# Eight weight chunks of the second block's modulation move from the first retrieval into the first mixer, and the retrieval's entry is reordered

## The chip, the cores and the metric

The kernel runs on one core of one Trainium2 chip, as one program. The time is device time in microseconds (us). Three timed runs of the kernel before gave 2483.28, 2483.88 and 2486.16 us; the median, 2483.88, is the number to compare. All arithmetic is float32.

## The reference, cut to what matters

Two blocks work on x, 256 tokens of width 1024, and a third part (sparse attention, gated linear attention and a mixture of experts) follows; the change does not touch that part. Each of the two blocks does:

```python
m = silu(c) @ mod_w[l] + mod_b[l]            # 6144 values: sh1, sc1, g1, sh2, sc2, g2
h = rms_norm(x, norm1_g[l]) * (1 + sc1) + sh1
y = mixer(h)                                 # l = 0: attention and gated MLP; l = 1: pooling
x = x + g1 * y
h2 = rms_norm(x, norm2_g[l]) * (1 + sc2) + sh2
x = x + g2 * peer_ffn(h2, ...)               # the retrieval
```

peer_ffn makes queries h2 @ w_q (2048 wide: 8 heads of two halves), scores them against 128 keys per half, takes the best 16 of the sums per head and token, and looks those 128 experts up in tables `down` and `up` of 16384 rows. The result of a token is the sum over its experts of gate times gelu(down_row . h2) times up_row. Each of the two blocks thus fetches 256 x 128 rows of 8 KB (a down and an up row side by side), 268 MB. The modulation weights of a block are 1024 x 6144, 25 MB, read for a single vector c.

## The kernel before, in words

Every engine has its own instruction stream, written out by hand, and they meet at semaphores. Weights come through a ring of four slots of 2 MB each; SyncE (SP) issues all weight loads in one fixed order, and before each load it waits until the last user of its slot is done (`load_weight`, L564 to L571). Which chunk goes to which slot is laid down by `stream(tag, chunks, used, places)`: `places` picks from the list `turn` of slots; without it the slot used longest ago is taken.

First comes a head (to 62 us) with four chunks of the first block's modulation. In the mixer the other eight chunks of that block are multiplied with silu(c) by `row_parts` (L2036): 16 instructions a chunk that put the chunk's result into row r of bank 7, where the rows add up in one accumulation. `cwin` is a window of zeros with c in one column; shifting it picks the row. VectorE then adds the bias rows to bank 7 (`mrows`, L1352), and eight matmuls with `rows_of(r)` (L2160) spread each row over the 128 partitions, from where ScalarE copies them to `mod`. Around it TensorE does the projections (`in_tiles`), attention in four iterations (scores1, turn1, value1) and the gated MLP; then `transposes` and `project_out1`, four products (two tiles of 128 tokens by two column halves) into banks 4 to 7.

`peer(0)` is the first retrieval. VectorE adds a tile to x (`add_tile`) and normalises it (`start`, with ScalarE's sum of squares and root, `enter`), tile 0 then tile 1. TensorE transposes a tile (`turn`), makes the query of the first two heads halved (`first_query`, `first_scores`), and then query products numbered s, each cut in four `quarter`s of 16 instructions and followed by `scores(s)`; number s stands for column chunk s // 2 and tile s % 2. Before the loop it does s = 1 and three quarters of s = 2. VectorE finds the top 16 in 15 steps (`top_k`); after head 0 the Pool engine starts fetching (L678), one indirect DMA for each expert number and tile: 128 tokens, 1 MB. There are 256 of them for each retrieval and eight buffers, four in the arena and two in each of two ring slots lent for the time (`lend`); number 6 waits for query product 1, and from number 8 on each pair waits until the matmuls of its buffer are done. For each pair VectorE makes two dot products (L1424), ScalarE applies gelu and the gate and builds two diagonal matrices (L888 to L897), and TensorE adds diagonal times up rows into the output banks (L2250), eight instructions. The quarters left over are spread over the first groups of this loop.

The second block's modulation is computed inside the retrievals: ten chunks in the first, two in the second (`HIDDEN`), one per block of eight pairs. `mod_parts` multiplies a chunk into bank 4 or 5, ScalarE copies it to `mpart`, `mod_total` sums over partitions and adds the bias, ScalarE copies it to `mod`. SyncE loads these chunks in between, waiting for the two slots that are not lent. `peer(1)` is the second retrieval, by the same code with l = 1.

## Time and profile before

| | |
|---|---|
| median of three timed runs | 2483.88 us |
| span of the profiled execution | 2487.9 us |
| TensorE (matmul) busy | 2124.6 us, 85% |
| VectorE busy | 1155.2 us, 46% |
| ScalarE busy | 648.8 us, 26% |
| Pool busy | 600.5 us, 24% |
| DMA, mean over the span | 347 GB/s, 864.07 MB |
| share of the gathers' queue (software_dynamic) | 536.90 MB, 52.3% of 16 engines |
| longest pieces of the chain that ended last | PE 50%, DMA 32%, DVE 7%, ACT 5% |

One execution was profiled; of it the page gives the span, from the first to the last instruction, and no other time. PE is TensorE, DVE VectorE, ACT ScalarE, POOL GpSimd, SP SyncE; PEclk is the clock granted to TensorE as a share of full speed. "Idle before" in a row is the time the engine stood still before that instruction, and behind the arrow stands what ended it.

### The profile page before, as it was taken

How to read it: one execution, taken by the hardware profiler on the slowest of the kernel's cores; microseconds unless marked ns; L12 is line 12 of the kernel's file. 1: busy time of each engine (PE TensorE's matmuls, PEld its weight loads, DVE VectorE, ACT ScalarE, POOL GpSimd, SP SyncE). 2: the span in 40 equal slices, each digit the busy share in tenths (PEclk: the TensorE clock that was granted, in tenths of full speed). 3: DMA queues.
4: the chain of work that ended last, by engine and by line, in shares of the span. 5: the costliest groups of instructions: out<-in, count | busy, mean ns of one | idle time of the engine just before them, and what ended most of it. 6: DMA issues, size and time to landing. Idle time of an engine off the chain costs nothing.

```text
span 2487.9 us, 21682 instructions
## 1 busy us (share of the span) xinstructions
PE 2124.6 (85%) x7687; PEld 1015.1 (41%) x7687; DVE 1155.2 (46%) x2838; ACT 648.8 (26%) x1824; POOL 600.5 (24%) x516
## 2 busy tenths in 40 slices
PE   7999898777777888898787777669998899999997
PEld 2556554332223336554332232224555444444442
DVE  1344765565565555765676667443425211111111
ACT  2242323332332322333332333231342110000001
POOL 0001443443434440444444444420000000000000
PEclk8999999998998999999999999989998899999999
DMA  8363999999999994999999999984221479999995
GB/s 354 136 277 144 414 412 415 419 422 411 421 421 412 415 420 182 421 419 415 420 420 411 420 410 420 421 342 191 85 89 75 172 304 427 426 428 428 426 428 221
DMA packets 98758, 864.07 MB, mean 347 GB/s; under 512 B 11196, under 2 KB 11324, under 8 KB 13400
## 3 DMA queue, kind: packets, MB, share of 16 engines
q0 software_dynamic: 73728, 536.90, 52.3%
q1 hardware_dynamic: 24920, 325.75, 31.5%
q8 instruction: 63, 1.03, 0.2%
q14 instruction: 47, 0.39, 0.0%
HBM read 861.57 MB, written 1.05 MB: 347 GB/s over the span
## 4 chain that ended last, share of the span: by engine, by line
PE 50%; DMA 32%; DVE 7%; ACT 5%; issue 3%; POOL 3%; POOLq 0%; SPq 0%; DVEq 0%; ACTq 0%
DMA ring<-in_experts,arena 28%; PE bank L1902 17%; PE bank L2250 13%; PE bank L2552 8%; PE bank L2595 4%; DVE ring L1424 3%; POOL ring L678 2%; PE bank L2562 2%; DMA arena<-in_experts,arena 2%; DMA arena<-in_w_up 2%; ACT arena L897 2%; ACT arena L892 1%; PE bank L2036 1%; PE bank L1953 0%; ACT arena L888 0%
## 5 line engine op out<-in xcount | busy, mean ns | idle before, releaser
L2250 PE MATMUL bank<-ring,arena 128*128 128x512 f32 x1024 | 493.7, 629 | 161.8 <-ACT arena L897 161.6
L2250 PE MATMUL bank<-arena 128*128 128x512 f32 x1024 | 484.5, 618 | 105.6 <-ACT arena L897 105.6
L678 POOL DMA_INDIRECT arena<-in_experts,arena x256 | 296.5, 1158 | 661.0 <-PE bank L2250 331.9
L1424 DVE SCALAR_TENSOR_TENSOR ring<-ring,h 128x1024 f32<-128x1024 f32 x256 | 313.9, 1226 | 297.8 <-DMA ring<-in_experts,arena 297.1
L1424 DVE SCALAR_TENSOR_TENSOR arena<-arena,h 128x1024 f32<-128x1024 f32 x256 | 313.6, 1225 | 210.1 <-DMA arena<-in_experts,arena 208.8
L678 POOL DMA_INDIRECT ring<-in_experts,arena x256 | 303.9, 1187 | 384.2 <-PE bank L2250 343.1
L2250 PEld LDWEIGHTS bank<-ring,arena 128*128 128x128 f32 x1024 | 195.2, 200 | 445.5 <-ACT arena L897 241.5
L2250 PEld LDWEIGHTS bank<-arena 128*128 128x128 f32 x1024 | 190.3, 195 | 380.2 <-issue 198.2
L888 ACT ACTIVATE arena<-arena 128x2 f32<-128x2 f32 x256 | 52.1, 203 | 916.6 <-DVE ring L1424 486.1
L1902 PE MATMUL bank<-ring,hT 128*128 128x512 f32 (+2 forms) x608 | 255.2, 578 | 10.4 <-DVE arena L1657 4.8
L2552 PE MATMUL bank<-ring,arena 128*64 128x512 f32 x768 | 223.4, 592 | 3.2 <-DMA arena<-in_w_up 2.0
L897 ACT ACTIVATE arena<-const,arena 128x128 f32<-128x128 f32 x512 | 177.6, 394 | 8.3
L1902 PEld LDWEIGHTS bank<-ring,hT 128*128 128x128 f32 x608 | 116.9, 195 | 139.6 <-issue 126.4
L1866 DVE TENSOR_TENSOR arena<-arena,bank 128x512 f32<-128x512 f32 x16 | 11.0, 689 | 305.1 <-PE bank L2552 305.1
L1902 PEld LDWEIGHTS bank<-hT,ring 128*128 128x128 f32 x1024 | 123.6, 196 | 19.6 <-issue 17.7
L2552 PEld LDWEIGHTS bank<-ring,arena 128*64 128x64 f32 x768 | 71.5, 137 | 146.9 <-issue 145.5
L1902 PE MATMUL bank<-hT,ring 128*128 128x128 f32 x1024 | 125.6, 279 | 3.1 <-ACT hT L845 3.1
L892 ACT ACTIVATE arena<-arena 128x1 f32<-128x1 f32 x512 | 123.0, 287 | 8.4
L2595 PE MATMUL bank<-ring,arena 128*64 128x512 f32 x256 | 113.3, 595 | 9.1 <-DVE arena L1868 9.1
L2595 PE MATMUL bank<-arena 128*64 128x512 f32 x256 | 113.3, 595 | 0.0
L2552 PE MATMUL bank<-arena 128*64 128x512 f32 x256 | 112.9, 594 | 0.0
L1072 ACT ACTIVATE arena<-bank 128x512 f32<-128x512 f32 x32 | 17.4, 595 | 214.3 <-PE bank L1902 214.3
(429 smaller groups left out, 1773.8 us busy)
## 6 DMA issues: line engine op xcount, KB each, us to landing
ring<-in_w_gate SPq DMA_DIRECT2D x32, 2048.0 KB, 15.1
ring<-in_mod_w SPq DMA_DIRECT2D x24, 2048.0 KB, 11.9
ring<-in_w_up SPq DMA_DIRECT2D x16, 2048.0 KB, 16.9
arena<-in_w_up SPq DMA_DIRECT2D x16, 2048.0 KB, 21.8
ring<-in_w_down SPq DMA_DIRECT2D x16, 2048.0 KB, 11.5
arena<-in_w_down SPq DMA_DIRECT2D x16, 2048.0 KB, 16.0
ring<-in_w_in SPq DMA_DIRECT2D x9, 2048.0 KB, 7.3
ring<-in_peer_w_q SPq DMA_DIRECT2D x8, 2048.0 KB, 11.6
```

The costliest lines, as they stand in the source:

```text
L678: pool.indirect_dma_start(out=gslot(l, n), out_offset=None, in_=a["experts"], in_offset=bass.IndirectOffsetOnAxis(ap=idx_all[:, t, at:at + ...
L888: link(act_.activation(part, part, ACT.Gelu_apprx_tanh))
L892: ins = act_.activation(act[:, t, k:k + 1], act[:, t, k:k + 1], ACT.Copy, scale=gate[:, t, k:k + 1])
L897: ins = act_.activation(diag[:, PER * (j % 2) + k], ident, ACT.Copy, scale=act[:, t, at + k:at + k + 1])
L1072: act_.activation(xs[:, 4 * half:4 * half + 4].rearrange("p a b -> p (a b)"), bank[half][:, :], ACT.Copy).then_inc(S["x_sel_ev"], 1)
L1424: ins = v.scalar_tensor_tensor(out=row, in0=row, scalar=1.0, in1=h[:, t], op0=ALU.mult, op1=ALU.mult, accum_out=act[:, t, HEAD * hh + k:HE ...
L1902: ins = pe.matmul(dst, lhsT, rhs, start=i == 0, stop=i == len(pairs) - 1)
L2036: ins = pe.matmul(bank[7][32 * j:32 * j + 32, :], cwin[:, 2 * j + k, 31 - r:63 - r], slot(i)[:, 2 * j + k], start=r == 0 and k == 0, stop= ...
L2250: ins = pe.matmul(bank[2 * t + c][:, :], diag[:, PER * (j % 2) + k], row[:, 512 * c:512 * c + 512], start=j % (GROUPS // NT) == 0 and k == ...
L2552: ins = pe.matmul(bank[2 + j][CAP * k:CAP * k + CAP, :], xs[:, q, CAP * k:CAP * k + CAP], w_k[3 * k + j][:, q], start=q == 0, stop=q == KT ...
L2562: ins = pe.matmul(bank[4 + 2 * t + c][:, :], selT[:, t], ysb[:, c], start=i == 0, stop=i == PAIRS - 1, skip_group_check=True)
L2595: ins = pe.matmul(bank[c][CAP * k:CAP * k + CAP, :], hsel[:, f, CAP * k:CAP * k + CAP], w_k[3 * k + 2][:, f, 512 * c:512 * c + 512], start ...
```

## The change

Of the twelve modulation chunks of the second block, eight are now rows 8 to 15 of the accumulation in bank 7: rows 0 to 14 are spread over the mixer, row 15 stands between the first and the second first query of the retrieval. VectorE empties bank 7 twice, after row 7 and after row 15 (`mrows1`). The last four chunks stay in the retrievals, two in each, but as rows too (`late_row`), and all twelve results are spread with one matmul each (`mod_total`) in the first retrieval (ten) and in the second (two). The slots of the mixer's loads are dealt anew. The biases come in one load. Most of the tensor `rows` is loaded after the second retrieval, since its place holds the two sums until then; the load of the band constants waits for row 15.

At the entry of the first retrieval the fourth product of `project_out1` comes after the first scores; tile 1 is added and normalised after VectorE's 15 selection steps, and ScalarE's part of it stands behind `score_out(1)`. In both retrievals the query products are renumbered (`QUERY`): before the loop come s = 1 (chunk 1, tile 0), its scores, the transposes of tile 1, all of s = 2 (chunk 0, tile 1) and its scores. Gather 6 waits for product 2 now, and in the first retrieval gather 4 waits for the fourth output product.

```diff
+ROWS = 16
+LATE = [{SHADOW: 8, SHADOW + 1: 9}, {SHADOW: 10, SHADOW + 1: 11}]
+TOTALS = [{SHADOW + 1 + c: c for c in range(10)}, {SHADOW + 3: 10, SHADOW + 4: 11}]
+QUERY = [(0, 0), (1, 0), (0, 1), (1, 1), (2, 0), (3, 0), (2, 1), (3, 1)]
+QUARTERS = {3 * (i // 2) + i % 2: (3 + i // 4, i % 4) for i in range(20)}
...
+        stream("rows", [mod_row(r) for r in range(15)], lambda r: ("modp", 4 + r + 1), (0, 0, 1, 0, 1, 0, 2, 1, 0, 2, 1, 0, 3, 2, 1))
+        stream("out1", [dealt("attn_out_w", c) for c in range(2)], lambda c: ("pout1", 3 + c), (0, 3))
+        stream("wq0", [dealt("peer_w_q_0", 0)], query_used(0), (2,))
+        stream("row_last", [mod_row(15)], lambda r: ("modp", 4 + 15 + 1), (1,))
+        stream("wq0_more", [dealt("peer_w_q_0", c) for c in (1, 2)], lambda i: query_used(0)(i + 1), (1, 0))
...
@@ SyncE
-            load_weights("mod0_rest", 8)
+            load_weights("rows", 15)
             load_weights("out1", 2)
-            load_weights("wq0", 2)
-            sp.wait_ge(S["mod"], 16)
+            load_weights("wq0", 1)
+            load_weights("row_last", 1)
+            load_weights("wq0_more", 2)
+            sp.wait_ge(S["rows_made"], 2)
             sp.dma_start(const[:, band_at:CONST_W], a["const"][:, band_at:CONST_W]).then_inc(S["in_const"], 16)
...
-            load_mod1_bias(0)
-            load_weights("mod1", 6)
...
+            load_weights("late0", 2)
...
             load_weights("in2", 2)
+            sp.dma_start(rows[:, 8:ROW_W], a["rows"][:, 8:ROW_W].to_broadcast([P, ROW_W - 8])).then_inc(S["in_rows"], 16)
             load_weights("in2_third", 1)
@@ Pool
+                    elif n == 4 and l == 0:
+                        pool.wait_ge(S["pout1"], 4)
                     elif n == 6:
-                        pool.wait_ge(S["pq"], query_no(l, 1))
+                        pool.wait_ge(S["pq"], query_no(l, QUERY.index((0, 1))))
@@ ScalarE, peer(l)
                 enter(0)
                 turned_out(0)
                 turned_out(1)
-                enter(1)
+                if l:
+                    enter(1)
                 head_out(0)
                 head_out(1)
-                turned_out(2)
-                turned_out(3)
                 gate_out(0, 0)
                 query_out(1)
                 score_out(1)
+                if l == 0:
+                    enter(1)
+                turned_out(2)
+                turned_out(3)
+                query_out(2)
+                score_out(2)
@@ VectorE, peer(l)
-                add_tile(1, (6, 7) if l == 0 else (2, 3), mod[:, 2], ("pout1", "py_pool")[l], "x_mix")
-                start(1)
+                if l:
+                    add_tile(1, (2, 3), mod[:, 2], "py_pool", "x_mix")
+                    start(1)
...
                 for step in range(STEPS):
                     top_k(0, step, 0, 1)
+                if l == 0:
+                    v.wait_ge(S["modp"], 4 + ROWS)
+                    v.tensor_tensor(mrows1, bank[7][:, :], mbias, ALU.add).then_inc(S["rows_made"], 1)
+                    add_tile(1, (2, 3), mod[:, 2], "pout1", "x_mix")
+                    start(1)
@@ TensorE, mixer
+            row_parts(0)
...
-            row_parts(0)
+            row_parts(1)
...
-            row_parts(1)
+            row_parts(2, 3)
+            between = {(1, 1): 6, (1, 3): 7, (2, 1): 10, (2, 3): 11, (3, 1): 13, (3, 3): 14}
...
-                    if it == 3 and p < 3:
-                        row_parts(5 + p)
+                    if (it, p) in between:
+                        row_parts(between[it, p])
                 if it == 0:
                     in_tiles(5)
-                    row_parts(2)
+                    row_parts(4, 5)
                 elif it == 1:
-                    in_tiles(6, 7)
-                    row_parts(3)
+                    in_tiles(6)
+                    row_parts(8)
+                    in_tiles(7)
+                    row_parts(9)
                 elif it == 2:
-                    row_parts(4)
+                    row_parts(12)
...
-            project_out1()
+            project_out1(0, 0)
+            project_out1(0, 1)
+            project_out1(1, 0)
@@ TensorE, peer(l)
                 first_scores(0)
+                if l == 0:
+                    row_parts(15)
                 first_query(1)
                 first_scores(1)
+                if l == 0:
+                    project_out1(1, 1)
+                for k in range(4):
+                    quarter(1, k)
+                scores(1)
                 turn(1)
                 for k in range(4):
-                    quarter(1, k)
-                for k in range(EARLY):
                     quarter(2, k)
-                    if k == 0:
-                        scores(1)
+                scores(2)
...
-                    if i == 7:
-                        for c in hidden(l, g):
-                            mod_parts(c)
-                    if i == 3:
-                        for c in hidden(l, g - 1):
-                            pe.wait_ge(S["in_modb"], 64 * (2 + c // 4 + l))
-                            mod_total(c)
+                    if i == 7 and g in LATE[l]:
+                        late_row(l, LATE[l][g])
+                    if i == 3 and g in TOTALS[l]:
+                        mod_total(TOTALS[l][g])
```

## Rows read from the trace of the kernel before

**Rows 1.** The page's slices: the span in 40 equal parts of 62.2 us.

```profile
GB/s 354 136 277 144 414 412 415 419 422 411 421 421 412 415 420 182 421 419 415 420 420 411 420 410 420 421 342 191 85 89 75 172 304 427 426 428 428 426 428 221
```

**Rows 2.** Stretches: start:end length, busy us of each engine, PEclk, DMA share, GB/s.

```profile
130.00:190.00 60.00, 56.67 (x345) 36.21 (x342) 25.07 (x52) 26.45 (x50) 0.00 (x0) 0.97 0.74 298
190.00:233.00 43.00, 40.30 (x195) 26.09 (x194) 20.30 (x54) 7.91 (x16) 1.23 (x2) 1.00 0.13 49
233.00:948.00 715.00, 581.17 (x1697) 262.01 (x1697) 435.25 (x1029) 221.01 (x705) 295.92 (x255) 0.95 1.00 410
991.00:1663.00 672.00, 538.26 (x1515) 244.27 (x1513) 429.29 (x1022) 211.04 (x685) 301.36 (x255) 0.97 0.99 411
...
295.00:300.00 5.00, 5.00 (x7) 2.00 (x6) 4.22 (x13) 2.03 (x6) 0.00 (x0) 0.50 1.01 421
```

**Rows 3.** Timeline of Pool: start us, length us, instruction, idle before and its releaser.

```profile
231.47 1.08 POOL L678 DMA_INDIRECT arena<-in_experts,arena  x1 [231.02 <-DVE arena L1408]
...
247.17 1.79 POOL L678 DMA_INDIRECT arena<-in_experts,arena  x1 [4.70 <-PE bank L2250]
...
988.87 0.94 POOL L678 DMA_INDIRECT arena<-in_experts,arena  x1 [57.67 <-DVE arena L1408]
...
1004.73 0.94 POOL L678 DMA_INDIRECT arena<-in_experts,arena  x1 [4.70 <-PE bank L2250]
...
1628.30 0.94 POOL L678 DMA_INDIRECT arena<-in_experts,arena  x1 [2.16 <-PE bank L2250]
...
1633.28 0.94 POOL L678 DMA_INDIRECT arena<-in_experts,arena  x1 [2.21 <-PE bank L2250]
```

**Rows 4.** Timeline of TensorE: expert matmuls of the two retrievals.

```profile
294.41 6.75 PE L2250 MATMUL bank<-arena 128*128 128x512 f32 x8 [4.47 <-ACT arena L897]
...
944.35 3.70 PE L2250 MATMUL bank<-ring,arena 128*128 128x512 f32 x8 [1.25 <-ACT arena L897]
...
1000.75 3.70 PE L2250 MATMUL bank<-arena 128*128 128x512 f32 x8 [2.37 <-ACT arena L897]
...
1659.16 3.70 PE L2250 MATMUL bank<-ring,arena 128*128 128x512 f32 x8 [1.26 <-ACT arena L897]
```

**Rows 5.** Chain of waits in the mixer: start us, length us, what.

```profile
110.31 1.85 PE bank L2036 x16
```

**Rows 6.** Timeline of TensorE: row and value products in the mixer.

```profile
156.12 2.69 PE L1902 MATMUL bank<-arena 128*128 128x64 f32 x16 [1.92 <-ACT arena L811]
158.75 2.83 PE L2036 MATMUL bank<-ring,const 128*32 128x512 f32 x16
```

**Rows 7.** DMA issues between 60 and 130 us: count, size, median us to landing.

```profile
ring<-in_mod_w SPq DMA_DIRECT2D x6, 2048.0 KB, 7.4
```

**Rows 8.** Timeline of TensorE: output products, turn, first query, quarters.

```profile
186.47 27.70 PE L1902 MATMUL bank<-ring,hT 128*128 128x512 f32 x64
214.01 1.04 PE L2184 MATMUL bank<-const,h 128*128 128x128 f32 x8
215.88 3.81 PE L1902 MATMUL bank<-hT,ring 128*128 128x128 f32 x32 [0.83 <-ACT hT L845]
...
227.37 9.20 PE L1902 MATMUL bank<-hT,ring 128*128 128x128 f32 x80 [0.74 <-ACT hT L845]
```

**Rows 9.** Timeline of VectorE: tile 0 added and normalised.

```profile
200.55 0.69 DVE L1143 TENSOR_TENSOR arena<-bank,arena 128x512 f32<-128x512 f32 x1 [5.45 <-PE bank L1902]
...
205.19 1.22 DVE L1136 TENSOR_TENSOR h<-h,arena 128x1024 f32<-128x1024 f32 x1
```

**Rows 10.** Timeline of ScalarE: squares, table change, first weighing.

```profile
215.74 1.06 ACT L710 ACTIVATE h<-x 128x1024 f32<-128x1024 f32 x1
...
227.33 1.28 ACT L870 ACT_TABLE_LOAD   x1
228.63 0.22 ACT L870 ACTIVATE arena<-arena 128x16 f32<-128x16 f32 x1
...
999.26 0.20 ACT L888 ACTIVATE arena<-arena 128x2 f32<-128x2 f32 x1 [2.51 <-DVE arena L1424]
```

More of the change, by code:

```diff
@@ L130, in selections @@
     return 9 * l + (m + 1 if m else head) + 1
-def hidden(l, g):
-    c = HIDDEN[l].start + g - SHADOW
-    return [c] if c in HIDDEN[l] else []
 PER = 2
@@ L415, in query_load, with row_load @@
         def query_load(l, c):
-            return wat[f"wq{l}"] + c if c < 3 else wat[f"wq{l}_last"]
-        def mod_load(c):
-            first = ("mod1", 0) if c < 10 else ("mod1_rest", 10)
-            return wat[first[0]] + c - first[1]
+            if c == 3:
+                return wat[f"wq{l}_last"]
+            return wat["wq0_more"] + c - 1 if l == 0 and c else wat[f"wq{l}"] + c
+        def row_load(r):
+            return wat["rows"] + r if r < 15 else wat["row_last"]
         def z_load(c):
@@ L1344, in _ @@
             out1(1)
+            v.wait_ge(S["in_mbias"], 32)
+            v.wait_ge(S["modp"], 12)
+            v.tensor_tensor(mrows, bank[7][:, :], mbias, ALU.add).then_inc(S["rows_made"], 1)
             softmax1(3)
@@ L1924, in transposes, with project_out1 @@
                     ins.then_inc(S["turned"], 1)
-            def project_out1():
-                for t in range(NT):
-                    pe.wait_ge(S["turned_ev"], turned("tcat", 2 * t + 2))
-                    for c in range(2):
-                        i = wat["out1"] + c
-                        wait_weight(pe, i)
-                        accumulate(bank[4 + 2 * t + c][:, :], [(tile(hT[:, q], t), slot(i)[:, q]) for q in range(KT)]).then_inc(
-                            S["pout1"], 1)
+            def project_out1(t, c):
+                pe.wait_ge(S["turned_ev"], turned("tcat", 2 * t + 2))
+                i = wat["out1"] + c
+                wait_weight(pe, i)
+                accumulate(bank[(4, 2)[t] + c][:, :], [(tile(hT[:, q], t), slot(i)[:, q]) for q in range(KT)]).then_inc(
+                    S["pout1"], 1)
             def project(tag, first, widths, ready):
@@ L1955, in quartered, with late_row @@
                 return ins
[L1957 to L1972 removed]
+            def late_row(l, c):
+                i, r = wat[f"late{l}"] + c % 2, 8 + c
+                wait_weight(pe, i)
+                for k in range(2):
+                    for j in range(4):
+                        ins = pe.matmul(bank[7][32 * j:32 * j + 32, :], cwin2[:, 2 * j + k, 31 - r:63 - r], slot(i)[:, 2 * j + k],
+                                        start=c % 2 == 0 and k == 0, stop=c % 2 == 1 and k == 1, skip_group_check=True)
+                ins.then_inc(S["modp"], 1)
+            def mod_total(n):
+                pe.wait_ge(S["rows_made"], 2 if n < 8 else 3 if n < 10 else 4)
+                if n:
+                    pe.wait_ge(S["mod_ev"], 16 + n)
+                pe.matmul(bank[6][:, :], rows_of(8 + n), mrows1 if n < 8 else mrows2, start=True, stop=True).then_inc(S["mod"], 1)
             def rows_of(r):
@@ L2218, in first_scores @@
                 def first_scores(hh):
-                    if l == 0:
-                        pe.wait_ge(S["x_mix"], NT)
                     pe.wait_ge(S["pq_ev"], 9 * l + hh + 1)
                     for k in range(2):
-                        ins = pe.matmul(tile(bank[6 + hh], k), qb[:, 0, 2 * hh + k], keysT[:, l, k], start=True, stop=True)
+                        ins = pe.matmul(tile(bank[6], 2 * hh + k), qb[:, 0, 2 * hh + k], keysT[:, l, k], start=True, stop=True)
                     ins.then_inc(S["ps"], 1)
```

114 lines of the change are left out of this document (43 added, 71 removed).

## The prediction

> **What bounds the kernel now.** I read the page's slices first, then stretches, then the timelines of the engines at the stage borders. The slices show 410 to 420 GB/s from about 250 us to 930 us and again from 1000 us to 1620 us, and 136 to 277 in the three slices before that [rows 1]. By stretches: the first retrieval (233 to 948 us) moves 410 GB/s with the DMA engines at 1.00 while TensorE is busy 581 of 715 us; the second (991 to 1663) is the same picture; the mixer's second half (130 to 190) has TensorE at 57 of 60 us and DMA at 0.74, and the mixer's exit and the entry of the retrieval (190 to 233) have DMA at 0.13 [rows 2]. So the mixer is TensorE's and the retrievals are DMA's. Late in the second retrieval the Pool queue starts a pair of gathers each 4.98 us (1628.30, 1633.28) [rows 3], and in that period TensorE works 3.7 us and waits for the rest [rows 4]: two gathers of 1.05 MB each in 4.98 us are 421 GB/s, the pace of the full DMA engines. Anything that takes bytes out of a retrieval gives time back, as long as the gathers start as early and never run dry. The reader should hold on to this condition; the change touches both sides of it.
>
> **Eight chunks leave the first retrieval.** Each is 2.1 MB, as much as a pair of gathers, so 4.98 us: 8 x 4.98 = 39.8 us. A second estimate: from its first gather to the end of its last expert matmul the first retrieval takes 231.47 to 948.05 = 716.6 us, the second 988.87 to 1662.86 = 674.0 [rows 3, 4]. The first carries ten modulation chunks, the second two, and one gain vector more (0.5 MB, 1.2 us): (42.6 - 1.2) / 8 = 5.2 us each, 41.4 in all. I take 39.8, bounds 39.8 to 42.7. With them go 8 chunk products (16 matmuls each) of TensorE, ScalarE's evacuations and 12 small bias loads: all work beside a full DMA, worth nothing.
>
> **Seven more rows before the mixer's end.** Rows 0 to 14 are now accumulated where 0 to 7 were. One is 16 matmuls and 1.85 us in the chain of waits [rows 5]; TensorE is the mixer's bound, so 7 x 1.85 = 13.0 us. But row 10 falls where TensorE waited 1.92 us for ScalarE (before 156.12), and after that wait the clock was low: the row at 158.75 lasts 2.83 us, 0.9 to 1.0 more than the one in the chain, and the value products of 2.69 us ahead of it lose, I estimate, as much [rows 5, 6]. Filling the gap returns 1.9 + 1.9, and 0.4 of a shorter wait next to it: +8.8 us (bounds 8.8 to 13). Each row's slot is refilled only after the row before in it is used. Alone, such a load lands 7.4 us after its issue [rows 7]; queued behind another it should follow 5.0 us later. Walking the queue: the sixth input tile ends at 127.5 + 3.7 (two rows more before it) = 131.2, so row 6 lands at 138.5, rows 7 to 14 follow each 5.0 us up to 178.5, and TensorE wants them at 141.1, 145.2, 151.2, 156.9, 164.3, 168.5, 170.4, 175.8 and 179.9. All in time, but by only 1.3 to 2.7 us for most. VectorE's new copy of bank 7 (0.7 us) sits behind out1(1) and is done by 148, before row 8 at 151.
>
> **The entry of the first retrieval.** Four output products took 27.6 us, 6.9 each [rows 8]. The fourth moves behind the first scores: -6.9. Turn 0 then starts at 214.0 + 8.8 - 6.9 = 215.9; tile 0 is normalised by then (6.0 us after its second product, 200.5 to 206.4 [rows 9], so 215.1). The path from there to the first indices is as before, so the first gather starts at 231.47 + 1.9 = 233.4 us (bounds -1 to +6 for the shift). The fourth product ends at 236.5 (first query 3.8, row 15 1.85, second query 3.8, 6.9 [rows 8]), and gathers 4 and 5, which now wait for it, are hardly late.
>
> What comes next is late. Tile 1 now goes: quarter product s=1, 64 matmuls at 9.2/80 each = 7.4 us [rows 8], to 243.9; query and score evacuation, to 246.2; only then ScalarE's squares (1.06 and 0.1), a change to the root's table (1.28 [rows 10]) and the root, to 249; VectorE's two passes of 1.2 us [rows 9] and small steps, to 251.6. VectorE's queue holds the whole dot products behind it, though the rows of gathers 0 to 5 are in. TensorE turns tile 1 at 252.6 after 7 us idle, and does quarter s=2 in 7.4 us (10.3 at the low clock: eight expert instructions took 6.75 us after a 4.47 us wait, 3.70 otherwise [rows 4]; the clock after that wait was 0.50, its lower level [rows 2]). Gathers 6 and 7 wait for this product: 262 to 265 us, instead of 1.2 us behind their neighbours. Then scores, their evacuation, the Gelu table and the first weighing (1.5 us from ScalarE's start to the matmul, 999.26 to 1000.75 [rows 4, 10]), and the first expert matmuls run 270 to 274 or 277. Gather 8 starts there, against 247.17 [rows 3].
>
> The DMA engines have six gathers (15 us) and the band constants (1 MB, 2.5 us, formerly loaded in an idle stretch) until 253, then nothing to 264 or 267, two gathers, and nothing again to 272 or 278 when gather 8's data flow. Idle 14 to 20 us; I take 18. Bounds 12 (all at full clock, dot products quicker) to 30 (low clock and a late pair in the loop too). After that TensorE owes the same number of quarters per group as the DMA allows time for, and I add 1 (0 to 3).
>
> A page of the Trainium skill bears on it: "ScalarE: Activation LUTs", section "What ACT_TABLE_LOAD costs", counts a drain of about 1.4 us with the 1.28 us of each table change. The trace disagrees: the load at 227.33 begins and the next instruction starts at once behind it [rows 10]. By the page's figure the added change would cost 1.4 us more, and the sum would be that much worse.
>
> **The second retrieval** gets the same order (s=1, scores, turn 1, whole s=2) but keeps tile 1's norm early. One quarter product (1.84) and two evacuations (0.6 each) more, plus turn 1 and its evacuations now in line: first expert matmuls 1006.4 instead of 1000.75, gather 8 at 1010.4 or, at the low clock, 1013.6 instead of 1004.73 [rows 3, 4]. Eight gathers last 20 us from 991 to 1011, data flow 2 us after an issue, by my estimate from the slices at the first entry, so 1.5 to 5 us of idle DMA: +3 (0 to 6).
>
> **At nothing:** the two late rows and twelve totals (TensorE has 1.3 us idle in each pair of gathers; without that 1.85 us each); VectorE's zeroing and additions (VectorE busy 435 of 715 us [rows 2]); the rows reload (0.6 MB, 1.4 us) ahead of the third input chunk, which TensorE wants 45 us later.
>
> **Sum**, against the span of the profiled execution, 2487.9 us, the only time the page gives for it: -39.8 (chunks) + 1.9 (mixer and moved product) + 2.5 (constants) + 18 (dry DMA) + 1 + 3 = -13.4 us, span 2474.5. The three timed runs have their median at 2483.88, 4.0 below that span; I carry the difference over: 2470.5 us. All bounds at their best give -42.7 - 1 + 2.5 + 12 = -29; at their worst -39.8 + 6 + 2.5 + 30 + 3 + 6 = +8.
>
> **The rivals.**
> Larger gain: -13.4 - 6 - 3 - 1.6 = -24 us, 2460. ScalarE and VectorE clear tile 1 faster than I walked and TensorE stays at full clock, so 12 us dry instead of 18, none in the second entry, and 5.2 us per chunk. For it: these engines are idle in that stretch. Against it: gather 8 must still wait for a queue of eight steps that I can name.
> No change: -13.4 + 10 = -3 us, 2481. The dry time is 28: TensorE at its low clock from the turn of tile 1 through the first expert groups. For it: the waits of 4.47 us and even of 1.92 us were followed by slow matmuls [rows 4, 6]. Against it: 2.37 us before 1000.75 were not [rows 4]. The page "TensorE: Matmul & The Clock Gate" of the Trainium skill (Part 1) names idleness as what throttles the clock to 1.2 GHz; the trace's 0.50 after the wait agrees [rows 2].
> Slower, by the loads of the mixer: +7 us, 2491. If rows 6 to 14 landed 7.4 us apart, the lone load's time [rows 7], and not 5.0, the ninth would be 9 x 2.4 = 21.6 late, less 1.5 of slack: +20. It breaks even at 6.6 us apart. Against it: a second load is queued behind each in my walk, and the stretch 130 to 190 already reaches 298 GB/s with waits between [rows 2].
> Slower, the change not doing what it says: if the first retrieval were held by the loop gather, dot, weigh, matmul, and not by bytes, the chunks would return nothing and the entry's 26 would stay: 2510. Against it: the second retrieval runs that loop with the chunks gone, 42.6 us faster.
>
> **Chances.** My forecast 0.55, larger gain 0.15, no change 0.15, slower by the loads 0.11, slower by the loop 0.04. Under 0.2% (5 us) a change cannot be told from none here. My forecast's case itself spreads some 6 us to each side, so nearly all of it is faster: faster 0.70, within 0.2% 0.16, slower 0.14. The range of 2457 to 2487 leaves the two slower cases and a corner of the largest gain outside.
>
> **What would show it.** Right: first gather near 233; gathers 6 and 7 near 263 and gather 8 near 274 to 277; a hole in the DMA between 253 and 278; first retrieval about 698 us long, ending near 931; row products up to 14 with no wait for a DMA ahead of them; second retrieval 3 us longer. Wrong: waits of TensorE for ring loads between 140 and 182 (the loads); first gather later than 240 (the mixer's stalls were not filled); gather 8 before 262 (larger gain) or after 285 (no change); a period above 5 us per pair with the chunks gone (the loop).

## The result, and the profile after

The changed kernel took 2470.59 us (median; 2465.80 to 2473.68), the kernel before beside it on the same chip 2486.16 us (2483.28 to 2488.66): a ratio of 0.9938, 95% interval 0.9922 to 0.9955. Forecast were 2470.5 us and a gain of 13.4; measured is a gain of 15.6.

One execution of that measurement, the profiled one, ran at a granted clock of 0.55 to 0.56 from beginning to end (span 3609.1 us), and one of old_entry below took 3100.74 us at 0.648; both are left out of the comparisons, and all rows of the kernel after come from a second measurement of it, labelled after_again.

> The changed kernel itself, to have an undisturbed profile of it. Theory (the prediction's walk): first gather near 233 us; gathers 6 and 7 near 263; gather 8 at 274 to 277 us; a hole in the DMA between 253 and 278 us; first retrieval about 698 us from first gather to last expert matmul, ending near 931; TensorE never waits for a ring load in the mixer; second retrieval about 677 us. Rival (loads): waits of TensorE for ring loads between 140 and 182 us, the first gather later than 240. Rival (loop): a pair of gathers takes more than 5 us late in the first retrieval. Time near 0.994 of the kernel before in all of them, since the time is known.

Measured: 2471.53 us against 2485.13, ratio 0.9951 (0.9933 to 0.9968). The span of its profiled execution is 2469.0 us, against 2487.9 before: 18.9 less, more than the medians differ. I account for those 18.9.

The page's slices of the kernel after, to be held against [rows 1]. Columns as there.

```profile
GB/s 347 194 379 221 283 420 420 420 421 419 416 412 415 418 378 218 389 413 422 420 419 420 420 416 421 415 346 191 99 88 55 200 303 426 427 427 428 427 427 220
```

The mixer's slices (third and fourth) rise from 277 and 144 to 379 and 221; the slice that holds the entry (the fifth, about 247 to 309 us) falls from 414 to 283; the fall between the retrievals begins a slice sooner (the fifteenth, 420 to 378). The stretches say it more sharply: start:end, length, busy us of each engine, PEclk, DMA share, GB/s, for the kernel after.

```profile
130.00:190.00 60.00, 59.75 (x414) 34.65 (x413) 23.93 (x51) 22.99 (x44) 0.00 (x0) 1.00 0.98 413
...
245.00:250.00 5.00, 0.03 (x1) 0.00 (x0) 1.84 (x4) 3.12 (x5) 0.00 (x0) 0.74 1.02 423
250.00:255.00 5.00, 3.28 (x14) 2.88 (x15) 4.86 (x16) 1.19 (x2) 0.00 (x0) 0.50 0.62 256
255.00:260.00 5.00, 5.00 (x35) 5.00 (x35) 4.83 (x17) 0.00 (x0) 0.00 (x0) 0.74 0.00 0
260.00:265.00 5.00, 4.13 (x35) 3.75 (x33) 4.74 (x15) 0.74 (x2) 1.45 (x2) 1.00 0.00 0
265.00:270.00 5.00, 1.74 (x2) 0.84 (x3) 0.65 (x1) 4.81 (x15) 0.84 (x1) 0.79 0.90 310
270.00:275.00 5.00, 5.00 (x23) 3.15 (x22) 4.54 (x12) 1.30 (x6) 1.28 (x1) 0.87 0.27 110
275.00:280.00 5.00, 5.00 (x25) 3.09 (x24) 0.18 (x1) 0.92 (x4) 2.15 (x3) 1.00 0.77 274
```

The first line answers to [rows 2]: six row products more (11 instead of 5) and 6.9 MB more (413 instead of 298 GB/s), a little over three loads, in the same 60 us, with TensorE at 59.75 instead of 56.67 us, its clock at 1.00 instead of 0.97, the DMA engines at 0.98 instead of 0.74. The others show the hole: 5 us times (1 - share), summed over the six lines from 250 on, is 17.2 us of idle DMA. Before, none of these slices is under 1.01.

The second retrieval has a smaller hole, behind its first gathers:

```profile
990.00:995.00 5.00, 5.00 (x21) 2.96 (x20) 4.66 (x14) 1.38 (x5) 1.00 (x1) 0.85 0.67 277
995.00:1000.00 5.00, 5.00 (x24) 3.09 (x24) 2.96 (x9) 1.38 (x5) 1.94 (x2) 1.00 0.85 280
```

Taken in slices of 1 us it is 3.1 us; the kernel before has no such slice behind its gathers of the second retrieval.

The Pool queue's gathers of the first retrieval in the kernel after (start, length, idle before and its releaser), against [rows 3]:

```profile
232.88 1.07 POOL L673 DMA_INDIRECT arena<-in_experts,arena  x1 [232.43 <-DVE arena L1400]
...
239.35 0.94 POOL L673 DMA_INDIRECT ring<-in_experts,arena  x1 [0.31 <-issue]
263.25 1.35 POOL L673 DMA_INDIRECT ring<-in_experts,arena  x1 [22.96 <-PE bank L1906]
264.90 0.94 POOL L673 DMA_INDIRECT ring<-in_experts,arena  x1 [0.30 <-issue]
273.72 1.56 POOL L673 DMA_INDIRECT arena<-in_experts,arena  x1 [7.88 <-PE bank L2263]
```

And TensorE's way to those two releases, the product of gather 6 and the expert matmuls of gather 8 (against [rows 4, 8]):

```profile
194.81 20.84 PE L1906 MATMUL bank<-ring,hT 128*128 128x512 f32 x48
215.48 1.04 PE L2194 MATMUL bank<-const,h 128*128 128x128 f32 x8
...
228.99 7.03 PE L1906 MATMUL bank<-ring,hT 128*128 128x512 f32 x16
235.86 7.31 PE L1906 MATMUL bank<-hT,ring 128*128 128x128 f32 x64
...
251.04 1.97 PE L2194 MATMUL bank<-const,h 128*128 128x128 f32 x8 [6.01 <-DVE h L1127]
253.69 9.28 PE L1906 MATMUL bank<-hT,ring 128*128 128x128 f32 x64 [0.69 <-ACT hT L833]
263.66 1.16 PE L2216 MATMUL bank<-cols,arena 128*128 128x128 f32 x8 [0.69 <-ACT arena L838]
...
268.26 5.19 PE L2263 MATMUL bank<-arena 128*128 128x512 f32 x8 [3.44 <-ACT arena L891]
```

The 6.01 us wait ends with VectorE's normalisation of tile 1 (L1127). What stood ahead of it is on ScalarE's timeline of the kernel after:

```profile
243.20 0.60 ACT L838 ACTIVATE arena<-bank 128x512 f32<-128x512 f32 x1 [12.10 <-PE bank L1906]
245.06 0.60 ACT L852 ACTIVATE arena<-bank 128x512 f32<-128x512 f32 x1 [1.26 <-PE bank L2216]
245.56 1.05 ACT L705 ACTIVATE h<-x 128x1024 f32<-128x1024 f32 x1
...
246.71 1.28 ACT L710 ACT_TABLE_LOAD   x1
248.00 0.20 ACT L710 ACTIVATE stat<-stat 128x1 f32<-128x1 f32 x1
```

VectorE had the last half of tile 1 added by 237.6:

```profile
236.85 0.74 DVE L1135 TENSOR_TENSOR x<-x,arena 128x512 f32<-128x512 f32 x1
```

ScalarE stood idle for 12.1 us before 243.20. For the first 6.5 of them tile 1 was not there yet; from 237.6 on its squares could have run, but they stood behind two evacuations that had nothing to evacuate yet, and began at 245.56, 8.0 us late.

The last expert matmuls of the first retrieval and the first ones of the second, kernel after, against [rows 4]:

```profile
926.40 3.70 PE L2263 MATMUL bank<-ring,arena 128*128 128x512 f32 x8 [1.25 <-ACT arena L891]
...
988.42 5.22 PE L2263 MATMUL bank<-arena 128*128 128x512 f32 x8 [3.44 <-ACT arena L891]
...
1643.12 3.70 PE L2263 MATMUL bank<-ring,arena 128*128 128x512 f32 x8 [1.23 <-ACT arena L891]
```

The account of the span, stretch by stretch, taking as borders the first gather of a retrieval and the end of its last expert matmul:

| stretch | before | after | difference | forecast |
|---|---|---|---|---|
| to the first gather | 231.47 | 232.88 | +1.4 | +1.9 |
| first retrieval | 716.6 | 697.2 | -19.4 | -18.3 |
| between the two | 40.8 | 40.7 | -0.1 | 0 |
| second retrieval (first gather 970.83) | 674.0 | 676.0 | +2.0 | +3 |
| the rest | 825.0 | 822.2 | -2.8 | 0 |

The last line is put down to the noise of single profiles. The change touches this part only by the load of the tensor `rows` and by two waits. In the eight profiles with the changed loads this stretch takes 821.8 to 827.1 us, in the two without them (before, before_cut) 825.0 and 832.6.

### The profile page after: what moved, and what is told of

It is laid out like the page before. It is cut to its first block, busy times and chain, and to the rows that moved or that the text cites. A ratio compares the mean times of both kernels' runs of the same rounds, so it can differ in the third digit from the quotient of the medians.

```text
span 3609.1 us, 21602 instructions
## 1 busy us (share of the span) xinstructions
PE 3519.5 (98%) x7663; PEld 1333.1 (37%) x7663; DVE 1159.8 (32%) x2843; ACT 647.7 (18%) x1813; POOL 583.3 (16%) x516
## 3 DMA queue, kind: packets, MB, share of 16 engines
HBM read 861.56 MB, written 1.05 MB: 239 GB/s over the span
## 4 chain that ended last, share of the span: by engine, by line
PE 97%; DVE 1%; ACT 1%; issue 1%; DMA 0%; SPq 0%; DVEq 0%; ACTq 0%
PE bank L2263 43%; PE bank L1906 25%; PE bank L2562 11%; PE bank L2605 6%; PE bank L2572 3%; PE bank L2040 1%; PE bank L1915 1%; PE bank L2216 1%; PE bank L1974 1%; PE bank L2106 0%; PE bank L1927 0%; PE bank L1955 0%; PE bank L2116 0%; PE bank L2168 0%; PE bank L1965 0%
## 5 line engine op out<-in xcount | busy, mean ns | idle before, releaser
L2263 PE MATMUL bank<-arena 128*128 128x512 f32 x1024 | 803.2, 967 | 6.9 <-ACT arena L891 6.9
L2263 PE MATMUL bank<-ring,arena 128*128 128x512 f32 x1024 | 801.0, 967 | 0.0
L1906 PE MATMUL bank<-ring,hT 128*128 128x512 f32 (+2 forms) x608 | 441.2, 916 | 4.4 <-DVE arena L1311 1.6
L2263 PEld LDWEIGHTS bank<-arena 128*128 128x128 f32 x1024 | 232.7, 230 | 530.4 <-issue 522.8
L2263 PEld LDWEIGHTS bank<-ring,arena 128*128 128x128 f32 x1024 | 232.0, 229 | 528.2 <-issue 528.2
L2562 PE MATMUL bank<-ring,arena 128*64 128x512 f32 x768 | 397.2, 967 | 1.2 <-ACT arena L1063 1.2
L1906 PEld LDWEIGHTS bank<-hT,ring 128*128 128x128 f32 x1024 | 202.1, 281 | 51.5 <-issue 48.6
L1906 PE MATMUL bank<-hT,ring 128*128 128x128 f32 x1024 | 206.7, 389 | 2.9 <-ACT hT L833 2.9
L2605 PE MATMUL bank<-ring,arena 128*64 128x512 f32 x256 | 199.6, 963 | 6.1 <-DVE arena L1872 6.1
L2562 PE MATMUL bank<-arena 128*64 128x512 f32 x256 | 200.6, 967 | 0.0
L2605 PE MATMUL bank<-arena 128*64 128x512 f32 x256 | 199.6, 962 | 0.0
L1906 PEld LDWEIGHTS bank<-arena,h 128*128 128x128 f32 x512 | 100.7, 288 | 18.4 <-issue 18.4
```

The lines of the kernel that those rows point to most:

```text
L1906: ins = pe.matmul(dst, lhsT, rhs, start=i == 0, stop=i == len(pairs) - 1)
L2263: ins = pe.matmul(bank[2 * t + c][:, :], diag[:, PER * (j % 2) + k], row[:, 512 * c:512 * c + 512], start=j % (GROUPS // NT) == 0 and k == ...
L2562: ins = pe.matmul(bank[2 + j][CAP * k:CAP * k + CAP, :], xs[:, q, CAP * k:CAP * k + CAP], w_k[3 * k + j][:, q], start=q == 0, stop=q == KT ...
L2605: ins = pe.matmul(bank[c][CAP * k:CAP * k + CAP, :], hsel[:, f, CAP * k:CAP * k + CAP], w_k[3 * k + 2][:, f, 512 * c:512 * c + 512], start ...
```

## The experiments

**before_cut: what eight chunks are worth.** The kernel before, with the first eight loads of the second block's modulation cut to 32 columns of one row group (their products read stale weights, so the second block's modulation is not computed):

```diff
+                if wat["mod1"] <= i < wat["mod1"] + 8:
+                    sp.dma_start(slot(i)[:, 0:1, 0:32], loads[i][:, 0:1, 0:32]).then_inc(w_landed[slots[i]], 16)
+                    return
```

> The kernel before, with the loads of the second block's first eight modulation chunks cut to one row group of 32 columns (128 bytes a partition instead of 16 KB); every matmul, copy and wait stays, so only 16.8 MB of the first retrieval's bytes go, and the modulation of the second block is left wrong. Theory (the retrieval is bound by bytes): 8 x 4.98 = 39.8 us less, up to 42.7, so about -41 us or a ratio of 0.9835; first retrieval 676 us long. Rival (the loop gather, dot, weigh, matmul is the bound): no more than -5 us.

Measured: 2443.95 us, ratio 0.9842 (0.9827 to 0.9856): 39 us by the ratio, 41 by the medians (2485.13 before). Its Pool queue starts the first gather at:

```profile
232.61 1.07 POOL L681 DMA_INDIRECT arena<-in_experts,arena  x1 [232.16 <-DVE arena L1411]
```

TensorE of the same kernel at the end of the retrieval:

```profile
905.00 3.70 PE L2253 MATMUL bank<-ring,arena 128*128 128x512 f32 x8 [1.26 <-ACT arena L900]
```

676.1 us instead of 716.6: the chunks are worth 40.5 us, 5.06 each. Every matmul, copy and wait is still there, so the first retrieval is paced by its bytes and not by the loop gather, dot, weigh, matmul. Of these 40.5 us the change keeps 19.4 in the first retrieval; the other 21.1 are lost again at its entry, the load of the constants included.

**tile1_first: the hole at the entry.** One call moves: ScalarE's squares and root of tile 1 go ahead of the two evacuations.

```diff
-                query_out(1)
-                score_out(1)
                 if l == 0:
                     enter(1)
+                query_out(1)
+                score_out(1)
```

> The changed kernel with one move: in the first retrieval ScalarE's part of tile 1 (squares and root) stands before the evacuation of query product 1 and its scores, not behind them. Theory (the DMA runs dry because tile 1 waits for that queue): tile 1 normalised at 244 instead of 250.5, TensorE turns it at 245 without going idle and keeps the full clock, gathers 6 and 7 start near 254.6 instead of 263.3, gather 8 near 263.4 instead of 273.7; dry DMA about 7 us instead of 18, so -10 to -11 us against the changed kernel, ratio to the kernel before near 0.990. Rival (something else holds the gathers, the selection steps or the slots): gather 8 moves by less than 3 us and the time stays at 0.994 to 0.995.

Measured: 2461.65 us, ratio 0.9907 (0.988 to 0.9934), 9 to 10 us below the change's two medians, and 10.8 below turn_early (below), which was measured beside it and has the change's entry. By the ratios to the kernel before it is 8 to 11 us, and the intervals just overlap (the change 0.9922 to 0.9955 and 0.9933 to 0.9968), so the size rests on the trace. TensorE of this kernel at the entry:

```profile
242.48 1.04 PE L2194 MATMUL bank<-const,h 128*128 128x128 f32 x8
244.31 7.41 PE L1906 MATMUL bank<-hT,ring 128*128 128x128 f32 x64 [0.79 <-ACT hT L833]
...
257.01 6.13 PE L2263 MATMUL bank<-arena 128*128 128x512 f32 x8 [3.44 <-ACT arena L891]
```

Its Pool queue:

```profile
230.50 1.08 POOL L673 DMA_INDIRECT arena<-in_experts,arena  x1 [230.04 <-DVE arena L1400]
...
251.99 0.94 POOL L673 DMA_INDIRECT ring<-in_experts,arena  x1 [14.08 <-PE bank L1906]
...
263.41 0.94 POOL L673 DMA_INDIRECT arena<-in_experts,arena  x1 [8.75 <-PE bank L2263]
```

The 6 us wait ahead of the turn is gone and the product behind it runs at full clock (7.41 instead of 9.28). Gather 8 starts 32.9 us after the first instead of 40.8, and the retrieval takes 689.2 us instead of 697.2: 7.9 earlier, 8.0 shorter. In slices of 1 us the idle DMA at the entry falls from 17.8 to 9.5 us, where 7 was expected. The hole is the price, and it converts one to one.

**old_entry: the entry's order undone, the chunks still moved.** All four output products first, tile 1 added and normalised in its old place; the query order stays.

```diff
             project_out1(1, 0)
+            project_out1(1, 1)
...
-                if l == 0:
-                    project_out1(1, 1)
...
-                if l:
-                    enter(1)
+                enter(1)
                 head_out(0)
                 head_out(1)
                 gate_out(0, 0)
                 query_out(1)
                 score_out(1)
-                if l == 0:
-                    enter(1)
...
```

(VectorE's `add_tile(1, ...)` and `start(1)` go back in front of the selection steps in the same way.)

> The changed kernel with the entry of the first retrieval in the old order: all four output products before the first turn, tile 1 added and normalised beside them; the rows, the late chunks and the numbering of the query products stay changed. Theory (the move of the fourth product costs more than it brings): first gather 6.9 us later, 239.8 instead of 232.9, but gather 6 at 253.5 and gather 8 near 262, before the DMA engines are done with the gathers ahead of them (264), so no dry time: first retrieval 679 us, its end near 919 instead of 930, -10 to -11 us against the changed kernel, ratio to before near 0.990. Rival (an earlier first gather is what counts): +6.9 us, ratio 0.997.

Measured: 2469.22 us, ratio 0.9926 (0.9902 to 0.9951); its interval overlaps that of the change, so the time alone shows no difference, where -10 to -11 us was expected. The trace tells more. First gather 237.73, 4.9 later, gather 8 at 268.00, 5.7 earlier, first retrieval ends at 924.2 instead of 930.1. There the direction was right and the size a little over half of what I expected; two new waits stood on the way. TensorE of this kernel:

```profile
236.35 7.41 PE L1900 MATMUL bank<-hT,ring 128*128 128x128 f32 x64 [2.36 <-DMA ring<-in_peer_w_q]
246.88 1.13 PE L2211 MATMUL bank<-cols,arena 128*128 128x128 f32 x8 [3.12 <-issue]
```

The first: the query weights of chunk 1 are loaded into the slot of row 15, so not before row 15 is used; in the change the fourth output product hides that load. The second wait is for ScalarE's evacuation of that product. The product ended at 243.8, and ScalarE began only at 246.19:

```profile
246.19 0.60 ACT L838 ACTIVATE arena<-bank 128x512 f32<-128x512 f32 x1 [10.25 <-remote]
```

In the change the evacuation begins at 243.20, right behind the product. Why ScalarE began 2.4 us late here stays open. What the run shows: the old order makes the first gather 4.9 us later and the way from it to gather 8 10.5 us shorter (30.3 instead of 40.8).

**weigh_first: the rest of the queue ahead of gather 8.** tile1_first, and the third query's scores and both evacuations (`query_out(2)`, `score_out(2)`, `scores(2)`) go behind the first expert matmuls, in both retrievals (`QUERIED[-1] = 2` puts the evacuations and scores there).

```diff
+QUERIED[-1] = 2
...
-                query_out(1)
-                score_out(1)
                 if l == 0:
                     enter(1)
+                query_out(1)
+                score_out(1)
                 turned_out(2)
                 turned_out(3)
-                query_out(2)
-                score_out(2)
...
                 for k in range(4):
                     quarter(2, k)
-                scores(2)
```

> tile1_first, and in both retrievals the scores of query product 2 go behind the first expert matmuls (ScalarE weighs pair 0 before it evacuates the product), as every later query product has it. Theory (the first expert matmuls wait for a queue of evacuations, not for rows): TensorE's wait of 3.44 us and the scores' 1.7 us leave the path, first expert matmuls 5 us earlier in both retrievals (24 to 26 instead of 26.5 us behind the first gather is the least, 21.5 the hoped), gather 8 likewise, first retrieval 683 to 684 us instead of 689.2, second 674 instead of 678.2, time -8 to -10 us against tile1_first, ratio to before 0.987. Rival (the second retrieval's 2 to 4 us come from elsewhere, and a dry DMA is made up for later): under 3 us, ratio 0.990.

Measured: 2454.83 us against 2487.72, ratio 0.9877 (0.9849 to 0.9906), span 2450.0: the fastest version, ahead of both kernels. By the ratios this is 7.5 us less than tile1_first, where -8 to -10 was expected. TensorE of this kernel at the entry:

```profile
245.37 7.41 PE L1905 MATMUL bank<-hT,ring 128*128 128x128 f32 x64 [0.79 <-ACT hT L834]
252.62 3.60 PE L2261 MATMUL bank<-arena 128*128 128x512 f32 x8
```

Its Pool queue:

```profile
231.56 1.07 POOL L674 DMA_INDIRECT arena<-in_experts,arena  x1 [231.11 <-DVE arena L1399]
...
253.06 1.17 POOL L674 DMA_INDIRECT ring<-in_experts,arena  x1 [14.06 <-PE bank L1905]
...
256.49 0.94 POOL L674 DMA_INDIRECT arena<-in_experts,arena  x1 [1.02 <-PE bank L2261]
```

No wait before the first expert matmuls, full clock, gather 8 24.9 us after the first. The first retrieval takes 681.2 us, the second 672.9 (first gather 952.40), where tile1_first took 689.2 and 678.2.

Four entries side by side (us, from unrounded times; idle DMA at the entry in slices of 1 us). The fourth column is nearly the same number four times:

| first retrieval of | gather 8 after the first | length | length less that | idle DMA |
|---|---|---|---|---|
| the change | 40.8 | 697.2 | 656.4 | 17.8 |
| tile1_first | 32.9 | 689.2 | 656.3 | 9.5 |
| old_entry | 30.3 | 686.4 | 656.2 | 7.8 |
| weigh_first | 24.9 | 681.2 | 656.3 | 3.5 |

The four other profiles with the change's entry give 655.8 to 657.2. Once the queue has run dry, what counts is when gather 8 starts; from there it is some 656 us to the end. The rule ends where the queue does not run dry: before_cut has gather 8 after 15.7 us and then takes 660.4, 676.1 in all. By these numbers (676.1 - 656.3), I estimate that a gather 8 up to about 20 us behind the first costs nothing. The second retrieval fits: 16.1 instead of 23.1 us, 7 us sooner, makes it only 3.1 us shorter.

**turn_early: is the second retrieval's loss the turn of tile 1?** In the second retrieval alone, the turn and its evacuations go ahead of product 1.

```diff
...
+                else:
+                    turn(1)
                 for k in range(4):
                     quarter(1, k)
                 scores(1)
-                turn(1)
+                if l == 0:
+                    turn(1)
```

> The changed kernel with the second retrieval alone changed back in one point: tile 1 is transposed and its transposes evacuated before query product 1, as in the kernel before. Theory: turn 1 (1.0 us) and its evacuation (about 0.8 and 0.7 of waits) leave the queue in front of query product 2, so gather 8 starts 1 to 2.5 us earlier than now (22 to 22.5 us behind the first gather instead of 23.1) and the second retrieval takes 674 to 675 us instead of 676.0: -1 to -2 us, hardly to be seen in the time. Rival (the new order costs nothing, the 2.0 us are something else): the second retrieval stays at 676.

Measured: 2472.43 us, ratio 0.9951 (0.9931 to 0.9971). TensorE at the second entry:

```profile
972.97 7.31 PE L1910 MATMUL bank<-hT,ring 128*128 128x128 f32 x64
...
985.57 5.90 PE L2270 MATMUL bank<-arena 128*128 128x512 f32 x8 [3.44 <-ACT arena L895]
```

The expert matmuls start 16.6 us after the first gather instead of 17.6, but last 5.90 us instead of 5.22, so gather 8 comes 22.7 us after the first instead of 23.1, the hole stays (3.0 us, it was 3.1), and the retrieval takes 677.6 us, no less than 676.0. My theory fell: taking the turn out alone wins nothing, since the slower matmuls took back 0.7 of the 1.0 us. What pays is everything between the third query product and the first expert matmuls together: the scores, two evacuations and the wait of 3.44 us with the clock after it. weigh_first takes them out of the way at both entries; its gather 8 comes 16.1 us after the first, its hole is 0.2 us, and its second retrieval is 5.3 us shorter than tile1_first's and 3.1 shorter than the change's. The runs do not separate the wait from the scores and the evacuations.

**loads_cut, rows_thin, rows_free: what paces the mixer.** The changed kernel, with the loads of rows 8 to 14 cut (loads_cut), with 14 of the 16 instructions of each of these rows left out (rows_thin), and both (rows_free). The second block's modulation is not computed in them.

```diff
+                if wat["rows"] + 8 <= i < wat["rows"] + 15:
+                    sp.dma_start(slot(i)[:, 0:1, 0:32], loads[i][:, 0:1, 0:32]).then_inc(w_landed[slots[i]], 16)
+                    return
...
+                            if 8 <= r < 15 and (k, j) != (1, 3):
+                                continue
```

> The changed kernel with rows 8 to 14 of the mixer cut to 2 of their 16 matmul instructions; their loads stay, and the modulation of the second block is left wrong. That takes 7 x 1.62 = 11.3 us of TensorE's work out of the mixer. Theory (a third of the rows' time only fills waits that ScalarE causes): the waits and the low clock behind them come back, first gather 7 to 8 us earlier than in the changed kernel (near 225), time -7 to -8 us. Rival (TensorE's work adds up in full): first gather 11.3 us earlier, near 221.5. Rival (the loads are what paces the rows): less than 5 us, with waits of TensorE for ring loads.

> The changed kernel with the loads of rows 8 to 14 cut to 128 bytes a partition, their products kept (the second block's modulation is left wrong). It asks whether the loads pace the mixer of the changed kernel. Theory (they land just in time, TensorE's work is the bound): no wait of TensorE to be taken away, the first gather stays within 1 us of the changed kernel's distance from the second input tile (232.88 - 63.07 = 169.8 us). Rival (the loads hold the rows up): that distance falls by 3 us or more.

> Both cuts at once: rows 8 to 14 with 2 of 16 matmul instructions and with the loads of 128 bytes (modulation of the second block left wrong). With the matmuls alone cut, TensorE waited for loads and the first gather came later, so this asks what the products cost TensorE once the loads cannot hold it. Theory (a third of the rows' 11.3 us only fills waits for ScalarE): first gather 7 to 8 us nearer to the second input tile than in the changed kernel, 162 to 163 us behind it. Rival (TensorE's work adds up in full): 158.5 us. If the low clock is what filled the difference, the waits' neighbours are long (2.7 instead of 1.9 us).

Measured: rows_thin 2472.35 us, ratio 0.9946 (0.9928 to 0.9965); loads_cut and rows_free, one execution each, 2471.08 and 2478.72 us. The head before the mixer varies by 3 us from profile to profile, so I count from the start of the second group of input products to the first gather (the change: 63.07 to 232.88; rows_thin: 61.88 to 236.51; loads_cut: 59.77 to 229.59; rows_free: 60.75 to 236.25):

| the change | loads_cut | rows_thin | rows_free |
|---|---|---|---|
| 169.8 | 169.8 | 174.6 | 175.5 |

Without the loads nothing changes: they do not pace the changed mixer. With most of the row products' instructions gone it gets 5 us *longer*, with the loads or without them; all profiles with the full rows and the change's entry (the change, tile1_first, weigh_first, turn_early, loads_cut) lie between 169.6 and 169.8, so this is far outside their spread. The theories and rivals of rows_thin and rows_free all had it otherwise. One of their terms was wrong from the start: the two instructions left of a row take 0.98 us up to the next group, where 16 take 1.85, so each thinned row saves 0.87 us and not 1.62, seven of them 6.1 us and not 11.3. TensorE of rows_free, up to the gated MLP's products (x32):

```profile
168.61 1.08 PE L1909 MATMUL bank<-arena 128*128 128x64 f32 x8 [1.69 <-DVE arena L1330]
...
174.71 3.52 PE L1909 MATMUL bank<-arena 128*128 128x64 f32 x16
...
180.00 7.09 PE L2094 MATMUL bank<-arena,cols 128*128 128x64 f32 x32
```

TensorE of the changed kernel, the same products:

```profile
177.80 1.95 PE L1906 MATMUL bank<-arena 128*128 128x64 f32 x16
...
181.53 3.79 PE L2089 MATMUL bank<-arena,cols 128*128 128x64 f32 x32
```

The stretch 170 to 190 of rows_free (PEclk is the third number from the end):

```profile
170.00:190.00 20.00, 20.00 (x70) 14.78 (x70) 4.99 (x10) 3.29 (x5) 0.00 (x0) 0.50 0.83 344
```

The same stretch of the changed kernel:

```profile
170.00:190.00 20.00, 19.75 (x144) 12.44 (x137) 7.51 (x17) 7.81 (x16) 0.00 (x0) 1.00 1.01 430
```

With the rows thinned TensorE waits for other engines (0.80 and 1.69 us), its clock falls from 1.00 to 0.50, its lower level, and the products there take almost twice as long: 7.09 for 3.79, 3.52 for 1.95. With the full row products the gaps are filled and the clock stays at 1.00. Whether the waits alone lowered it, or the thinned products as well, these runs do not separate. Nor is the loss in every execution: the profiled run of rows_thin took 2475.96 us, but the median of its ten is 2472.35, no more than the change's; five of them lie between 2463.2 and 2469.8 and five between 2475.0 and 2481.5. In rows_thin TensorE also waits for the loads (1.61, 0.20 and 1.47 us, with the DMA engines at 1.00): the margin that the prediction walked was thin indeed, and is used up as soon as the products get quicker.

## Why the prediction was right

That the time itself came out within 0.1 us of the forecast (2470.59 for 2470.5) is luck: the second measurement gave 2471.53, and the kernel before moved by 2.3 us between its medians. The terms are what can be held against the runs.

- **Chunks, -39.8:** right. before_cut gave -40.5.
- **Mixer and moved product, +1.9:** +1.4 measured, and 0.94 of it is already there when the input products start (63.07 against 62.13 before), in code that did not change. Counted from there, it is 169.34 before and 169.81 after: +0.5. The working was right in its places: the wait of 1.92 us is gone, rows 0 to 14 wait for no load, the fourth product ends at 236.0 (forecast 236.5). The 8.8 was some 1.4 too much, so the term was mis-sized, and the trace shows by what: a second stretch of low clock that I did not price. Behind the same wait of 2.14 us the input product took 8.80 us before and 7.11 after:

```profile
101.51 8.80 PE L1902 MATMUL bank<-ring,hT 128*128 128x512 f32 x16 [2.14 <-DVE arena L1320]
```

```profile
104.65 7.11 PE L1906 MATMUL bank<-ring,hT 128*128 128x512 f32 x16 [2.14 <-DVE arena L1311]
```

The first line is the kernel before, the second the one after; before_cut has 8.80 too, tile1_first 7.11. With it the term closes: 13.0 for seven rows, less 1.92 and 0.47 of waits, 1.64 of slow products behind the wait at 154 to 156 (2.69 and 2.83 instead of 1.96 and 1.92) and 1.69 here is 7.3; measured is 8.8 - 1.4 = 7.4. The rows cost less than their sum because the clock stays up: it was 0.94 in 100 to 130 and 0.86 in 150 to 160, and is 1.00 in both after. rows_free supports this from the other side.
- **The hole, 18:** right, 17.2 measured, and its two steps were hit: gathers 6 and 7 at 263.3 and 264.9 (262 to 265), gather 8 at 273.7 (274 to 277), tile 1's turn at 251.0 (252.6). tile1_first and weigh_first show the cause, since each step taken out of that queue came back one to one. The low clock was part of it as forecast (9.28 and 5.19 us), though milder than the worst case.
- **Constants, +2.5:** not measured alone. Something else was left out of the walk: the second of two query weight loads, issued together at 224.26 behind row 15, is still moving when the first gather starts. Between the borders of the first retrieval the engines move 278.82 MB instead of 293.50: 16.78 less for eight chunks, 1.05 more for the constants and 1.05 for half of that weight load. It cost nothing that the trace shows, as the engines were idle at that moment before (share 0.35 in 230 to 235) and are full now (1.02). With the forecast's own terms the first retrieval closes: -40.5 + 2.5 + 17.2 + 1 = -19.8, measured -19.4; the 2.5 and the 1 in it are not measured.
- **Second retrieval, +3:** +2.0 in this pair of profiles. All profiles together: 676.0, 676.1, 676.3, 677.1, 677.6, 677.9 and 678.2 with the new order, 674.0 and 672.9 with the old: +3.6. The mechanism is the one forecast, a late gather 8 and 1.5 to 5 us of idle DMA: gather 8 comes 23.1 us behind the first (forecast 21.5 or 24.7), and the hole is 3.1 us. Of its causes the turn is no lever by itself, as turn_early shows. The lengths with the new order spread by 2.2 us at equal holes (the change and tile1_first both 3.1); that stays open.
- **The rivals:** the larger gain needed an unbroken clock and a gather 8 before 262; it came only when the queue was rebuilt (weigh_first, 256.5). No change needed a hole of 28 us. The loads did land in time. The loop is not the bound: late gathers of the first retrieval still come each 4.98 us (900.53, 905.51).

The Trainium skill, "ScalarE: Activation LUTs", section "What ACT_TABLE_LOAD costs", would have added a drain of about 1.4 us to the table change. The added load at 246.71 lasts 1.28 us, the instruction ahead of it ends at 246.7 and the root starts at 248.00: this trace disagrees with the page again. For the clock, "TensorE: Matmul & The Clock Gate", Part 1, says that activity is what releases the throttle. rows_free agrees: with fewer row instructions and two waits the granted clock fell to 0.50.

The gain in the span (18.9) is larger than in the medians (15.6 and 13.6); the rest behind the second retrieval alone accounts for 2.8 of the span's.

## What to carry to other kernels

Bytes taken out of a stretch that is bound by transfers came back here at their full price (5 us for each 2.1 MB), but only while the queue of transfers stays fed: write down for each transfer what releases it, and walk that chain at the entry, where a gather that starts 8 us late cost 8 us once the queue had run dry. Put what releases the next transfer first in every engine's order, and evacuations that nobody is waiting for behind it: the squares of tile 1 behind two idle evacuations were worth 8 us of the hole, the third query's scores and evacuations ahead of the first expert matmuls another 8. Work added to a TensorE stage with gaps cost next to nothing here, and in two profiles work taken out cost time, because the clock was lower for up to 20 us behind the gaps.

## What the runs showed of the hardware

That removing matmuls can make a stage longer I had not expected: 98 row instructions less (7 rows, 14 of 16 each) went with a mixer 5.7 us longer (175.5 against 169.8 us) in the one execution of rows_free, with the clock at 0.50 where it had been 1.00. Nor that short waits weigh so unevenly: behind the same wait of 3.44 us, the eight expert instructions took 5.19, 5.22, 5.35, 5.40, 5.90 and 6.13 us in six places, 3.70 behind one of 2.37 [rows 4]. Four of the six (5.22, 5.35, 5.40, 6.13) had the same two groups just ahead, a product of 7.41 and scores of 1.16 us. So the value can be read off neither the wait nor the groups right before it; what sets it is not shown.
